# Two-layer decoder trunk on one core: six buffers for raw weight pieces in the FFN blocks, and a later load of the final norm's weight

## The reference

```python
h = x
for layer in range(DEPTH):                      # DEPTH = 2
    if layer < N_A_LAYERS:                      # layer 0
        h = h + gated_deltanet(rms_norm(h, mixer_norm_g[layer]), ...)
    else:                                       # layer 1
        h = h + nsa_attention(rms_norm(h, mixer_norm_g[layer]), shared_kv, ...)
    h = h + swiglu_ffn(rms_norm(h, ffn_norm_g[layer]), ffn_w_gate_up[layer], ffn_w_down[layer])
    if layer == N_A_LAYERS - 1:
        shared_kv = nsa_shared_kv(h, kv_norm_g, kv_w, ...)
return rms_norm(h, final_norm_g)

def swiglu_ffn(x, w_gate_up, w_down):
    gate, up = jnp.split(x @ w_gate_up, 2, axis=-1)
    return (jax.nn.silu(gate) * up) @ w_down    # hidden width FFN_HIDDEN = 5632
```

## Time and profile before

| | |
|---|---|
| median of 3 runs | 2913.34 us (2907.93 to 2913.54) |
| profiled execution | 2917.91 us |
| its span, first to last instruction | 2916.1 us |
| TensorE products busy / weight loads busy | 2785.1 us (96%) / 2293.4 us (79%) |
| VectorE / ScalarE busy | 2224.3 us (76%) / 1649.9 us (57%) |
| DMA from the stream | 912 transfers of 512 KB |
| mean granted clock of TensorE | 0.987 |

### The profile page before, as it was taken

One profiled execution on the slowest core, in us unless ns is written; L12 is line 12 of the kernel. 1 busy time (PEld: TensorE's weight loads), 2 busy tenths in 40 slices (PEclk: granted clock), 3 DMA queues, 4 the chain that ended last, 5 costly groups with the idle time before them and its releaser, 6 DMA issues.

```text
span 2916.1 us, 40678 instructions
## 1 busy us (share of the span) xinstructions
PE 2785.1 (96%) x13456; PEld 2293.4 (79%) x13456; DVE 2224.3 (76%) x2717; ACT 1649.9 (57%) x2179; POOL 30.4 (1%) x29
## 2 busy tenths in 40 slices
PE   8999999999979999999999999799999999999997
PEld 6878888888867787878787788688877888778776
DVE  5877877877866688888888854556667888888886
ACT  6766766667664555555555554544445555555554
POOL 0000000000000000000000000000000000000000
PEclk9999999999999999999999999799999999999999
DMA  6534544444424566666565655533345665656554
GB/s 236 176 129 145 166 151 144 161 157 149 160 80 127 162 197 189 198 192 198 193 194 183 200 177 189 165 123 111 106 130 195 200 192 190 194 183 194 190 190 149
DMA packets 135088, 493.13 MB, mean 169 GB/s; under 512 B 15008, under 2 KB 15328, under 8 KB 134624
## 3 DMA queue, kind: packets, MB, share of 16 engines
q1 hardware_dynamic: 133776, 487.82, 51.7%
q10 hardware_dynamic: 1232, 4.23, 0.4%
HBM read 489.86 MB, written 2.13 MB: 169 GB/s over the span
## 4 chain that ended last, share of the span: by engine, by line
issue 57%; PE 23%; DMA 8%; DVE 8%; ACT 2%; POOL 0%; DVEq 0%; SPq 0%; ACTq 0%; POOLq 0%
DMA RAW<-stream 8%; PE ACC L666 6%; PE ACC L668 5%; PE ACC L667 5%; DVE W_LO L1743 2%; PE SIDE L674 1%; DVE WORK L1765 1%; DVE W_LO L1496 1%; DVE H L1521 1%; PE SIDE L876 1%; ACT W_HI L1327 1%; PE SIDE L878 1%; PE SIDE L877 1%; DVE WORK L1759 1%; DVE W_LO L1739 1%
## 5 line engine op out<-in xcount | busy, mean ns | idle before, releaser
L1496 DVE TENSOR_TENSOR W_LO<-RAW,W_HI 128x1024 fp32r<-128x1024 f32 x424 | 513.2, 1222 | 337.1 <-ACT W_HI L1091 335.0
L1327 ACT ACTIVATE W_HI<-RAW 128x1024 fp32r<-128x1024 f32 x488 | 470.7, 987 | 303.8 <-PE ACC L668 175.3
L1091 ACT ACTIVATE W_HI<-RAW 128x1024 fp32r<-128x1024 f32 x424 | 442.4, 1056 | 228.3 <-PE ACC L668 201.8
L1743 DVE TENSOR_TENSOR W_LO<-RAW,W_HI 128x1024 fp32r<-128x1024 f32 x408 | 494.1, 1219 | 51.2 <-ACT W_HI L1327 46.9
L666 PE MATMUL ACC<-W_HI,X_HI 128*128 128x512 f32 x1216 | 489.5, 403 | 16.6 <-DVE W_LO L1496 16.3
L668 PE MATMUL ACC<-W_HI,X_LO 128*128 128x512 f32 x1216 | 475.9, 391 | 0.0
L667 PE MATMUL ACC<-W_LO,X_HI 128*128 128x512 f32 x1216 | 475.7, 391 | 0.0
L666 PE MATMUL ACC<-W_HI,A_HI 128*128 128x512 f32 x992 | 397.8, 401 | 9.4 <-issue 8.0
L668 PE MATMUL ACC<-W_HI,A_LO 128*128 128x512 f32 x992 | 389.9, 393 | 0.0
L667 PE MATMUL ACC<-W_LO,A_HI 128*128 128x512 f32 x992 | 389.3, 392 | 0.0
L1327 ACT ACTIVATE W_HI<-WORK 128x1024 fp32r<-128x1024 f32 x160 | 169.9, 1062 | 300.0 <-PE SIDE L878 230.1
(11 more groups left out here) (311 smaller groups left out, 3739.2 us busy)
## 6 DMA issues: line engine op xcount, KB each, us to landing
RAW<-stream SPq DMA_DIRECT2D x912, 512.0 KB, 4.5
WORK<-gdn_rows ACTq DMA_DIRECT2D x8, 512.0 KB, 5.9
WORK<-xt SPq DMA_DIRECT2D x4, 512.0 KB, 9.5
H<-x SPq DMA_DIRECT2D x2, 1024.0 KB, 13.3
out<-WORK SPq DMA_DIRECT2D x4, 512.0 KB, 3.9
WORK<-tails SPq DMA_DIRECT2D x2, 512.0 KB, 10.7
WORK<-gfin SPq DMA_DIRECT2D x1, 1024.0 KB, 7.3
K<-consts SPq DMA_DIRECT2D x1, 518.0 KB, 6.6
```

What stands on the lines that cost most here:

```text
L1091: nc.scalar.activation(W_HI[:, h % WS, :], raw_piece(h), ACT.Copy).then_inc(hi_ready, 1)
L1327: nc.scalar.activation(dst, src, ACT.Copy).then_inc(hi_ready, 1)
L1496: nc.vector.tensor_tensor(W_LO[:, h % WS, :], raw_piece(h), W_HI[:, h % WS, :].bitcast(f32), SUB).then_inc(lo_ready, 1)
L1743: nc.vector.tensor_tensor(lo, src, hi, SUB).then_inc(lo_ready, 1)
```

## The change

There are three parts.

- `RING` = 6 buffers take the pieces of iterations 1 to 10: the four of `RAW` and two in the work area, columns 2048 to 3071 and 3072 to 4095. Piece p goes to buffer p mod 6. The pieces of the plain iteration 0, of the last "d" slots (iteration 11) and of all other stages keep the ring of four. The new function `raw_at` gives the buffer, the semaphore and its count for ScalarE and VectorE.
- SyncE's loads of the blocks are written out for iteration 1 (its first four pieces wait as for four buffers), loop over iterations 2 to 10, and are written out for the last eight pieces.
- `final_norm_g` is loaded behind the last piece of the stream, as its place in the work area is now used by the ring.

```diff
+RING = 6
...
+        raw_more = [w(2048, 1024), w(3072, 1024)]
...
-        raw_full = [sem(f"raw_full{i}") for i in range(RAWS)]
+        raw_full = [sem(f"raw_full{i}") for i in range(RING)]
...
+        def raw_at(base, it, wrap, kind, piece):
+
+            if kind == "d" and wrap:
+                tile, sem_, n = raw_piece(piece), raw_full[piece % RAWS], 4 * (FBLK - 1) + piece // RAWS + 1
+                return tile, sem_, 16 * n + ffn_loads(base)
+            s = piece % RING
+            tile = RAW[:, s, :] if s < RAWS else raw_more[s - RAWS]
+            n = it * 64 + (64 * (wrap - 1) + 16 * (piece // RING + 1))
+            return tile, raw_full[s], n + (ffn_loads(base) if s < RAWS else 64 * (FBLK - 1) * (base == B_FFN1))
...
-                act.wait_ge(raw_full[piece % RAWS], (ffn_raw(base, it) + 24 * wrap) * (16 // RAWS) + 16 * (piece // RAWS + 1))
-                src = raw_piece(piece)
+                src, full, n = raw_at(base, it, wrap, kind, piece)
+                act.wait_ge(full, n)
...
                 for p in (piece, piece + 1):
-                    dve.wait_ge(raw_full[p % RAWS], (ffn_raw(base, it) + 24 * wrap) * (16 // RAWS) + 16 * (p // RAWS + 1))
+                    dve.wait_ge(*raw_at(base, it, wrap, kind, p)[1:])
...
             def feed_ffn(base, ob):
 
-                def next_piece(it, p):
-                    sp.wait_ge(lo_ready, ffn_c(ob, it) + (RAW_FREE[p - RAWS] + 1 if p >= RAWS else p - RAWS + 1))
-                    load_piece(it * 12 + (base - 4 + p // 2), p)
-
-                with sp.Fori(1, FBLK) as it:
+                def next_piece(it, p, free):
+                    tile, full, _ = raw_at(base, 1, 0, "", p)
+                    sp.wait_ge(lo_ready, ffn_c(ob, it) + free)
+                    at = p % 2 * PIECE
+                    sp.dma_start(tile, stream[it * 12 + (base - 4 + p // 2)][:, at:at + PIECE]).then_inc(full, 16)
+
+                free = [p - RING + 1 for p in range(RING)] + [RAW_FREE[p] + 1 for p in range(24 - RING)]
+                for p in range(24):
+                    next_piece(1, p, p - RAWS + 1 if p < RAWS else free[p])
+                with sp.Fori(2, FBLK) as it:
                     for p in range(24):
-                        next_piece(it, p)
+                        next_piece(it, p, free[p])
+                for p in range(8):
+                    sp.wait_ge(lo_ready, ffn_c(ob, FBLK) + 24 + (free[p] if p < RAWS else p - RAWS + 1))
+                    load_piece(base + C_FFN - 4 + p // 2, p)
 
             feed(RAWS, B_FFN0 + 8)
             feed_ffn(B_FFN0, O_FFN0)
-            feed(B_KV - 4, B_KV + 8, MORE)
+            feed(B_KV, B_KV + 8, MORE)
...
             feed(B_KV + 8, B_FFN1 + 8, MORE)
-            sp.wait_ge(w_used, O_FFN1)
+            feed_ffn(B_FFN1, O_FFN1)
             sp.dma_start(gfs, gfin).then_inc(fin_in, 16)
-            feed_ffn(B_FFN1, O_FFN1)
-            feed(CHUNKS - 4, CHUNKS, 2 * MORE)
```

More of the change, by code:

```diff
@@ L637, in ffn_raw, with ffn_loads @@
             return it * 24 + (2 * base - 8)
+        def raw_at(base, it, wrap, kind, piece):
[6 more added lines that the diff above has]
+            return tile, raw_full[s], n + (ffn_loads(base) if s < RAWS else 64 * (FBLK - 1) * (base == B_FFN1))
+        def ffn_loads(base):
+            return (2 * base + 16) * (16 // RAWS) - (32 * (FBLK - 1) if base == B_FFN1 else 0)
         def ffn_ahead(it, e):
@@ L1087, in split_hi @@
             more = surplus(c + h) if isinstance(c, int) else 0
-            act.wait_ge(raw_full[h % RAWS], (c - more if more else c) * (16 // RAWS) + 16 * (h // RAWS + 1))
+            act.wait_ge(raw_full[h % RAWS], (c - 2 * more if more else c) * (16 // RAWS) + 16 * (h // RAWS + 1))
             if not (isinstance(c, int) and c + h < WS):
@@ L1737, in ffn_lo @@
             hi, lo = W_HI[:, e % WS, :].bitcast(f32), W_LO[:, e % WS, :]
+            raw = raw_at(base, it, wrap, kind, piece)[0]
             if kind == "21":
-                nc.vector.tensor_tensor(lo[:, 0:COLS], raw_piece(piece)[:, COLS:2 * COLS], hi[:, 0:COLS],
-                                        SUB).then_inc(lo_ready, 1)
+                nc.vector.tensor_tensor(lo[:, 0:COLS], raw[:, COLS:2 * COLS], hi[:, 0:COLS], SUB).then_inc(lo_ready, 1)
             else:
-                src = {"13": t13, "24": t24}.get(kind, raw_piece(piece))
+                src = {"13": t13, "24": t24}.get(kind, raw)
                 nc.vector.tensor_tensor(lo, src, hi, SUB).then_inc(lo_ready, 1)
@@ L1751, in weight_sum @@
                 return
-            b11_22, b12_21 = raw_piece(piece), raw_piece(piece + 1)
+            b11_22, b12_21 = (raw_at(base, it, wrap, kind, p)[0] for p in (piece, piece + 1))
             done = sums_done(ph, it, wrap) + 3 * j
```

## The result

| | before | after |
|---|---|---|
| median | 2910.64 us (2904.87 to 2913.54, 4 runs) | 2886.29 us (2884.12 to 2889.58, 4 runs) |
| profiled execution / span | 2917.91 / 2916.1 us | 2889.58 / 2887.8 us |
| mean granted clock of TensorE | 0.987 | 0.986 |

The ratio is 0.992, 95% interval 0.990 to 0.994. Measured again, beside 17 runs of the kernel before, it was 0.9893 (0.9879 to 0.9907): 2886.48 against 2915.51 us. The change makes the kernel about 1% faster; 2885 us was forecast.

The account below looks back on a forecast made before the run. TensorE was taken to bound the FFN loops, its small idle remainder due to VectorE waiting for weight transfers. 27 + 1.2 = 28 us less gave 2890 us profiled, 2885 us median; range 2877 to 2901 for 8 in 10.

Parts of the forecast that it names:

- 1, the waits removed: FFN loops: six buffers end VectorE's waits for weight pieces and TensorE's stops behind them; 27 us gained, bounds 23 and 30.
- The 24.9 us of the stops: FFN loops: gain counted from TensorE's 34 listed stops, 17.0 us idle plus 5.4 and 2.5 us of slower products.
- The lead of 6.7 us: Third and fourth groups' "11"/"21" pair: 6.7 us from issue to need, against landings of 4.7, at most 6.5 us.
- What is late next: nothing: FFN loops: VectorE needs 56.4 of an iteration's 64.0 us, so nothing of its is late and TensorE sets the pace.
- 2, the place of the loads: Two of six buffers in the work area, first iteration written out: 0 us, bounds 0 and +0.5.
- rival C: Transfers into the work area slow VectorE's operations there; at 20% slower, 45 us more, 2958 us; chance 0.04.
- 3, the norm weight: Second FFN block's entry: moving this load cuts TensorE's 1.47 us stop to 0.27, 1.2 us gained; tail 0, bound +3.
- 4: Semaphore counts, scalar operations and the eight static loads at each block's end: 0 us.
- A: FFN loops: longer landings or a still late third and fourth groups' pair leave half the gain, 2899 us; chance 0.11.
- B: No change: TensorE's stops come back for another maker, such as ScalarE's high half; 2913 us; chance 0.05.
- D: More gain than forecast, sized by TensorE's weight loads' share: 38 us less, 2875 us; chance 0.05.
- Waited for by nobody's semaphore: TensorE's pause ahead of iteration 11: no semaphore is waited for there, and the pause stays after the change.

## Why the prediction was right

*Forecast.* 28 us less than the profiled execution, 2890, and 2889.58 was measured; 2885 for the median, and it is 2886.29. The mechanism is right, but a match within 1.5 us is in part luck. A fourth run moved the median of the kernel before from 2913.3 to 2910.6 us. The gain itself was 24.4 us between these medians and 29.0 between the repeated ones, and the four runs of the changed kernel span 5.5 us. In the profiled execution the blocks gained 29.8 us, not 27, and 1.5 us that were lost elsewhere bring it back to the forecast.

*1, the waits removed: right in place, a little small in size.* Predicted 26.0 us in the 18 periods, at 64.0 each; measured 28.1 us and 63.89. With 1.0 us for the first iterations it said 27, where the two blocks gained 29.8, near its upper bound of 30. The iteration taken as undisturbed, 64.0, still held about 0.1 us of short delays. The 24.9 us of the stops was the lower figure, as said, and short stops are the reason: from 1075 to 1640 us the kernel before has 31 products that start over 0.25 us after their forerunner with no wait listed, the changed one 9, which is 2.4 us more. The lead of 6.7 us held: in the loops the longest landing of their own loads is 6.1 us, and no wait of VectorE for the stream is left there. At the second block's entry two loads took 7.3 and 7.4 us, longer than the prediction's "at most 6.5", which was read inside the loop. "What is late next: nothing" is right for the kernel as changed. The runs with late "pa" and "pb" show a condition that the step did not name: its 6.7 us are counted from the moment the buffer is free, and that is the moment of the issue only while everything ahead in the queue is out. In the changed kernel it is.

*Why the pairs.* The step argued that the "11"/"21" pair carries the gain, and that the lead of the others only adds. Late pairs, with what stands behind them in the queue, do lose everything; but late "pa" and "pb" alone lose about half, and the waits of VectorE that they bring are waits for pairs held up in the queue. Its statement on the "d" pieces is right: late ones cost nothing.

*2, the place of the loads: 0, right.* The low halves by source, first loop, with count and mean ns, for the earlier trace rows:

```profile
L1759 DVE TENSOR_TENSOR W_LO<-WORK,W_HI 128x1024 fp32r<-128x1024 f32 x135 | 164.0, 1220 | 57.5 <-ACT W_HI L1343 57.5
L1759 DVE TENSOR_TENSOR W_LO<-RAW,W_HI 128x1024 fp32r<-128x1024 f32 x120 | 145.5, 1219 | 13.1 <-ACT W_HI L1343 12.9
```

1220 against 1219 ns, with pieces landing in the work area beside them. That answers rival C as well, and the rule that the Trainium skill gives (SBUF — State Buffer, SBUF: two separate sides) agrees with this trace. Pieces land about as fast in either place, too: in the first block's loop after 4.6 us in the work area and 4.7 in the ring, in the median.

*3, the norm weight: place right, size 0.3 us too large.* The entries of the two blocks, for the earlier trace rows:

```profile
1011.22 0.50 PE L682 MATMUL ACC<-W_HI,X_HI 128*128 128x512 f32 x1 [0.41 <-DVE W_LO L1512]
...
2204.37 0.50 PE L682 MATMUL ACC<-W_HI,X_HI 128*128 128x512 f32 x1 [0.58 <-DVE W_LO L1512]
```

The stop went from 1.47 to 0.58 us, 0.9 less where 1.2 was forecast; the other block's, taken for the fixed rest, itself moved from 0.27 to 0.41. Alone the edit can't be told from nothing. The late load landed in time: issued at 2851.79, landed after 6.6 us, first used at 2862.19 without a wait. VectorE's timeline there, for the earlier trace rows:

```profile
2861.05 1.23 DVE L1512 TENSOR_TENSOR W_LO<-RAW,W_HI 128x1024 fp32r<-128x1024 f32 x1
2862.19 1.22 DVE L1886 TENSOR_TENSOR WORK<-H,WORK 128x1024 f32<-128x1024 f32 x1
```

*4: 0, nothing in the trace speaks against it.*

*The rivals.* A needed landings over 8 us or a pair still late; neither came. B needed another maker of the stops; there is none. C is answered above. D rested on the weight loads' share, 34 us, against 28.1 in the periods. The reason that the prediction gave for the excess, shorter loads of the transposes, carries little of it: the undisturbed stretch of 10 us was 82.6% loaded, and the second loop, transposes and all, is 82.5%. With 485.76 us in place of 472.78 this share would still give 15.7 us for that loop, where the products counted give 14.1. The loads' busy time is itself not constant: the same 2860 loads were drawn 527.7 and 527.9 us long before and 529.8 and 529.6 after.

*The observations.* Waits at the first sum 60 to 2, as said. TensorE's stops in the loops 34 to 0 (said: under 5). Period 63.89 (said: 64.0 to 64.2), a small miss. Entry stop 0.58 (said: 0.3), the other one. Final weight not waited for, and the pause stays, both as said. "Waited for by nobody's semaphore" was wrong about the pause: it is the wait for VectorE's and ScalarE's halves, shown by the two runs that removed it.

## What to carry to other kernels

Price the removal of a recurring wait by the loop's period against an undisturbed iteration of the same trace, and use the listed stops only as the lower bound. A deeper ring helps by the moment at which each load leaves the queue: in an in-order queue an early load is as late as the latest one ahead of it, and loads released together also land late together, so read the issues of the queue beside the buffers. When such waits are gone, look at the next stop even where no releaser is named: the instructions that end right before it restarts are the suspects, and an edit that frees them tests it. Here a spare pair of tiles was worth another 0.4%.

## What was not expected of the hardware

Three transfers of 512 KB that went out within 1.4 us landed after 6.4, 7.7 and 8.4 us. Two that went out 2.3 us apart, at the same place of the loop, landed after 3.8 and 4.2 us. Over the first loop the median landing is 4.7 us (ring) and 4.6 (work area) in the changed kernel, and 5.1 and 5.8 us with late "pa" and "pb".

After the pause of 3.63 us TensorE ran at half its clock for some products: they step 0.43 us in place of 0.23, six between 2853.6 and 2855.8 us in the changed kernel, ten at the first pause. In the kernel before it was seven and eight. They began right at the restart in both cases of the changed kernel, and 0.6 and 1.5 us after it in the kernel before. The granted clock of the slow products, of the whole stretch behind the pause and of the next (the columns of the earlier trace rows):

```profile
2853.10:2855.70 2.60, 2.60 (x7) 2.01 (x7) 0.00 (x0) 0.00 (x0) 0.00 (x0) 0.50 0.99 321
2852.60:2857.70 5.10, 5.07 (x16) 4.11 (x17) 0.00 (x0) 0.48 (x1) 0.00 (x0) 0.68 0.84 304
2858.00:2863.00 5.00, 5.00 (x24) 4.14 (x23) 4.33 (x4) 1.67 (x3) 0.00 (x0) 1.00 0.00 0
```

The slow products run at 0.50, the lower of the two levels (1.2 GHz), and the stretch has 16 products against 24 in about 5 us. By the steps, the first products after the two pauses of the changed kernel took 2.5 and 1.6 us more than as many undisturbed ones, and the pauses 3.8 us each. That is 11.7 us, of which the clock is about a third, and the two versions without the pause save 10.6 and 10.8 us in the medians. With no pause, no such product is left at either place.
